# A 34,267-instruction, two-block transformer kernel: the first score products of four attentions placed between projections, and the last mixer's compressed scores computed with the keys stationary

## The reference, cut to what matters

```
# cross_attn, twice: 4 heads of 256
q = xn @ wq;  sc = q k^T * 256**-0.5;  p = softmax(sc);  o = p v;  h = h + o @ wo
# even_mixer_2: q, k (rotated), v for 8 causal heads, and 4 heads with two softmax maps each
qa, ka, va, qb, kb, vb = split(h @ w_in);  w = p[:, 0] - lam * p[:, 1]
# odd_mixer: 16 query heads, 4 key heads; three branches added under learned gates
s_c = q kc^T   # kc, vc: 15 compressed blocks, two small matrix products over 32 tokens each
p_c = softmax(mask(s_c));  o_c = p_c vc
o = g0 * o_c + g1 * o_selected + g2 * o_window
```

## Time and profile before

| | us |
|---|---|
| three runs | 2513.89, 2507.85, 2509.01 |
| median | 2509.01 |
| span of the profiled execution | 2503.7 |
| PE busy in it | 2362.8 |

### The profile page before, as it was taken

One profiled execution on the slowest core, in us unless ns is written; L12 is line 12 of the kernel. 1 busy time (PEld: TensorE's weight loads), 2 busy tenths in 40 slices (PEclk: granted clock), 3 DMA queues, 4 the chain that ended last, 5 costly groups with the idle time before them and its releaser, 6 DMA issues.

```text
span 2503.7 us, 34267 instructions
## 1 busy us (share of the span) xinstructions
PE 2362.8 (94%) x14928; PEld 1345.4 (54%) x14928; DVE 685.4 (27%) x1507; ACT 379.2 (15%) x812; POOL 1.2 (0%) x9
## 2 busy tenths in 40 slices
PE   7899999999999999989998999988979997989997
PEld 6767888877676333323333333335656334856433
DVE  2565122149555110101010101001142122263122
ACT  2002100010221111101110111101032111153212
POOL 0000000000000000000000000000000000000000
PEclk9899999999999999999998999998989998989999
DMA  9588154564374998999999999998402996542591
GB/s 314 185 299 313 68 215 155 194 220 140 108 262 178 351 382 330 390 370 393 394 393 393 394 394 359 387 370 328 146 34 72 324 339 168 146 135 73 194 346 50
DMA packets 328739, 645.07 MB, mean 258 GB/s; under 512 B 12907, under 2 KB 98177, under 8 KB 328577
## 3 DMA queue, kind: packets, MB, share of 16 engines
q1 hardware_dynamic: 325804, 637.63, 70.9%
q10 hardware_dynamic: 2773, 5.11, 0.6%
HBM read 641.66 MB, written 1.05 MB: 257 GB/s over the span
## 4 chain that ended last, share of the span: by engine, by line
PE 88%; DVE 7%; issue 3%; ACT 2%; ACTq 0%; DVEq 0%
PE bank L1579 22%; PE bank L1274 19%; PE bank L1644 11%; PE bank L1544 6%; PE bank L1498 6%; PE bank L1510 3%; PE bank L1571 3%; PE bank L1294 3%; DVE att L3276 2%; PE bank L1704 2%; PE bank L1663 1%; PE bank L1630 1%; PE bank L1790 1%; PE bank L1323 1%; PE bank L1724 1%
## 5 line engine op out<-in xcount | busy, mean ns | idle before, releaser
L1579 PE MATMUL bank<-ring,xn 128*32 128x512 f32 x3648 | 469.7, 595 | 0.0
L1274 PE MATMUL bank<-xn,ring 128*128 128x256 f32 x2048 | 451.8, 382 | 2.9 <-issue 1.0
L1274 PEld LDWEIGHTS bank<-xn,ring 128*128 128x128 f32 x2048 | 390.9, 192 | 60.7 <-issue 7.8
L1579 PEld LDWEIGHTS bank<-ring,xn 128*32 128x32 f32 x3648 | 128.6, 110 | 273.7 <-issue 270.0
L1644 PE MATMUL bank<-ring,att 128*32 128x512 f32 x2256 | 254.4, 593 | 1.3 <-ACT att L2326 1.3
L2883 DVE TENSOR_TENSOR sq<-att,bank 32x512 f32<-32x512 f32 x70 | 48.0, 686 | 501.2 <-ACT att L2337 351.9
L1544 PE MATMUL bank<-ring,xn 128*64 128x512 f32 x304 | 146.1, 627 | 28.2 <-issue 28.2
L1644 PEld LDWEIGHTS bank<-ring,att 128*32 128x32 f32 x2256 | 72.8, 110 | 162.5 <-issue 162.1
L1498 PE MATMUL bank<-xn,ring 128*128 128x256 f32 x704 | 152.8, 379 | 0.0
L1546 PE MATMUL bank<-ring,xn 128*64 128x512 f32 x304 | 147.3, 632 | 0.0
L1498 PEld LDWEIGHTS bank<-xn,ring 128*128 128x128 f32 x704 | 133.8, 190 | 18.3
(11 more groups left out here) (351 smaller groups left out, 2142.2 us busy)
## 6 DMA issues: line engine op xcount, KB each, us to landing
ring<-od_moe_gu SPq DMA_DIRECT2D x98, 2048.0 KB, 17.6
ring<-od_moe_down SPq DMA_DIRECT2D x49, 2048.0 KB, 15.6
ring<-ada_w SPq DMA_DIRECT2D x24, 2048.0 KB, 8.8
ring<-moe_w_gate SPq DMA_DIRECT2D x32, 1024.0 KB, 10.8
ring<-moe_w_up SPq DMA_DIRECT2D x32, 1024.0 KB, 10.5
ring<-moe_w_down SPq DMA_DIRECT2D x16, 2048.0 KB, 13.6
z<-od_moe_gu SPq DMA_DIRECT2D x14, 2048.0 KB, 18.7
ring<-ev_w_in SPq DMA_DIRECT2D x10, 2048.0 KB, 19.8
```

The source lines that it names most:

```text
L1274: mm = nc.tensor.matmul(ps[:, c * T:(c + 1) * T], kblk(b)[:, k, u * T + c * P:u * T + (c + 1) * P], x[:, k, :], start=k == 0, stop=k == KD ...
L1579: return nc.tensor.matmul(PSB[f.b][j * QP:(j + 1) * QP, :], src[:, k, at:at + QP], kblk(b)[:, k, :], start=k == 0, stop=k == KD - 1)
```

## The change

In both cross-attentions a score pass stands behind the next unit of the query projection, so that units and passes alternate on PE; ACT's copies and exponentials and DVE's `ada_step`s, reductions and normalisations alternate in the same way. In the even mixer the projections come in the order qa, ka, qb, kb, va, vb, the first unit's scores stand between the two halves of va and the second unit's ahead of vb; the wait for the last rotation is replaced by a wait of each unit for its own. The rotation's temporary moves from `sq` to `att`. In the last mixer the first unit's scores stand ahead of the `cmp_w2` products, the compressed scores are made as 8 products with the 32 key columns stationary and 256 query columns moving, in four column strips of a bank, ACT copies them, PE goes on with the second unit's scores, and four transposes bring the compressed scores into the layout of before. The score banks there become two fixed sets, (6, 7, 4) and (0, 1, 4), so that all units use bank 4 for the early tile. `turn_compressed` moves behind `turned(0)`.

```diff
-                j.s_fill, j.t_fill = fill((0, 1, 6)[i % 3]), fill(2 + i % 2, (probT_ready, count(probT_ready, 1) + 1))
+                j.s_fill, j.t_fill = fill((6, 7, 1)[i % 3]), fill(2 + i % 2, (probT_ready, count(probT_ready, 1) + 1))
...
+        SCORE_PAIRS = (6, 7, 4), (0, 1, 4)
...
+                freed = (score_ready, st.score + 3 * u.i + 3)
+                u.early_fill = fill(at[2], freed) if len(at) > 2 else fill_turn(freed)
+
+            def score_banks(u):
+                return pairs[u.i % 2] if pairs else [SCORE_BANKS[(3 * u.i + k) % 5] for k in range(3)]
...
         MW = MOBA_H * HD
-        ev2.ropes = [rope_linear(W2, 0, MW), rope_linear(W2, MW, MW)]
-        ev2.va = token_linear(W2, 2 * MW, MW, proj_ready)
-        ev2.ropes += [rope_linear(W2, 3 * MW, MW), rope_linear(W2, 4 * MW, MW)]
-        ev2.vb = token_linear(W2, 5 * MW, MW, proj_ready)
-        ev2.lam_fill = fill_turn()
...
-        ev2.att = maps(units, (att, kT.rearrange("p k t -> p (k t)")))
+        ev2.ropes = [rope_linear(W2, at * MW, MW) for at in (0, 1, 3)]
+        ev2.lam_fill = fill_turn()
+        ev2.ropes.append(rope_linear(W2, 4 * MW, MW))
+        ev2.att = maps(units, (att, kT.rearrange("p k t -> p (k t)")), begun=True)
+        ev2.va = token_linear(W2, 2 * MW, MW, proj_ready)
+        ev2.att.score_fills(units[0], (6, 7))
+        ev2.att.score_fills(units[1], (6, 7))
+        ev2.vb = token_linear(W2, 5 * MW, MW, proj_ready)
+        ev2.att.rest()
+        for i, u in enumerate(units):
+            u.rotated = (rope_ready, ev2.ropes[1 if i < 2 else 3].rope + i % 2 + 1)
+            u.projected = (proj_ready, (ev2.va if i < 2 else ev2.vb).end)
...
             u.evac = (slice(0, T), mixed[:, i, :])
+            u.rotated, u.projected = (rope_ready, od2.q.rope + i // 2 + 1), None
             units.append(u)
-        od2.cturn = fill(TURN_BANKS[1], (csoft_ready, od2.csoft + 4))
-        od2.att = maps(units, (att, z[:, 8:14, :].rearrange("p k t -> p (k t)")))
+        od2.att = maps(units, (att, z[:, 8:14, :].rearrange("p k t -> p (k t)")), begun=True, pairs=SCORE_PAIRS)
+        od2.att.score_fills(units[0], SCORE_PAIRS[0])
+        for i, st in enumerate(od2.cmp):
+            st.out = count(cmp_ready, 2)
+            st.ofill = fill_turn((cmp_ready, st.out + 2))
+        od2.csoft = count(csoft_ready, 4)
+        od2.by_block = fill(5, (blockwise_ready, 1))
+        od2.att.score_fills(units[1], SCORE_PAIRS[1])
+        od2.cscore = fill(5, (csoft_ready, od2.csoft + 1))
+        od2.att.rest(lambda: fill(TURN_BANKS[1], (csoft_ready, od2.csoft + 4)))
...
-            def pe_attention(st):
+            def pe_attention(st, q_unit):
+
                 def scores(j):
+                    pe.wait_ge(*j.projected)
...
                 js = st.jobs
-                for j in js[:3]:
-                    scores(j)
+                for i in range(len(js)):
+                    q_unit(i)
+                    if i:
+                        scores(js[i - 1])
+                scores(js[-1])
                 for i, j in enumerate(js):
-                    if i + 3 < len(js):
-                        scores(js[i + 3])
                     turned(j)
                     if i:
                         values(js[i - 1])
                 values(js[-1])
...
-                pe_linear(st.q, xn, normed(st.norm))
-                pe.wait_ge(proj_ready, st.q.end)
-                pe_attention(st.att)
+
+                def q_unit(i):
+                    b, u, f = st.q.units[i]
+                    if u == 0:
+                        landed(b)
+                    unit(b, u, f, xn, normed(st.norm) if i == 0 else None)
+                    sums_beside(st.q, i)
+
+                pe_attention(st.att, q_unit)
...
             rotate(r[0], 0)
-            pe_token_linear(ev2.va, xn)
+            pe_linear(r[2], xn, None)
             rotate(r[1], 4)
-            pe_linear(r[2], xn, None)
-            pe_linear(r[3], xn, None)
-            rotate(r[2], 8)
-            pe_token_linear(ev2.vb, xn)
-            rotate(r[3], 12)
             pe.wait_ge(lam_ready, 1)
             ps = open_bank(ev2.lam_fill)
             nc.tensor.matmul(ps[:, 0:2], ones[0:1, :], lam[0:1, 6:8], start=True, stop=True)\
                 .then_inc(bank_full[ev2.lam_fill.b], 1)
-            pe.wait_ge(rope_ready, r[3].rope + 2)
-            pe.wait_ge(proj_ready, ev2.vb.end)
-            pe_maps(ev2.att)
+            pe_linear(r[3], xn, None)
+            rotate(r[2], 8)
+            scores, rest = pe_maps(ev2.att)
+            for i, (b, c, f) in enumerate(ev2.va.units):
+                if i == 0:
+                    landed(b)
+                else:
+                    scores(ev2.att.units[0])
+                token_unit(b, c, f, xn)
+            rotate(r[3], 12)
+            scores(ev2.att.units[1])
+            pe_token_linear(ev2.vb, xn)
+            rest()
...
+            scores, rest = pe_maps(od2.att)
+            pe.wait_ge(dup_ready, od2.kv[1].dup + 2)
+            scores(od2.att.units[0])
...
+            ps = open_bank(od2.by_block)
+            for half in range(2):
+                for q in range(4):
+                    i = 4 * half + q
+                    g = i // 2
+                    mm = nc.tensor.matmul(ps[q * QP:(q + 1) * QP, half * T:(half + 1) * T],
+                                          kcmp[:, g // 2, g % 2].rearrange("p h n -> p (h n)"), z[:, i, :],
+                                          start=True, stop=True)
+            mm.then_inc(bank_full[od2.by_block.b], 1)
+            scores(od2.att.units[1])
+            pe.wait_ge(blockwise_ready, 1)
             ps = open_bank(od2.cscore)
             for c in range(TC):
-                for i in range(NSA_H // 2):
-                    g = i // 2
-                    at = c * T + i * 2 * NCMP_PAD
-                    mm = nc.tensor.matmul(ps[:, at:at + 2 * NCMP_PAD], z[:, i, c * P:(c + 1) * P],
-                                          kcmp[:, g // 2, g % 2].rearrange("p h n -> p (h n)"), start=True, stop=True)
+                for half in range(2):
+                    mm = nc.tensor.transpose(ps[:, c * T + half * P:c * T + (half + 1) * P],
+                                             raw_cmp[:, half, c * P:(c + 1) * P], ident)
             mm.then_inc(bank_full[od2.cscore.b], 1)
-            pe.wait_ge(dup_ready, od2.kv[1].dup + 2)
...
-            pe_maps(od2.att, turn_compressed)
+                mm.then_inc(bank_full[od2.att.second.b], 1)
+
+            rest(turn_compressed)
...
                 js = st.jobs
+                q_unit(0)
+                q_unit(1)
                 exps(js[0])
+                q_unit(2)
                 exps(js[1])
+                q_unit(3)
...
             copy_units(r[0], pairs(z), HD ** -0.5)
             copy_units(r[1], pairs(z, 4))
-            copy_units(ev2.va, tokens())
             copy_units(r[2], pairs(z, 8), HD ** -0.5)
             copy_units(r[3], pairs(z, 12))
+            exps, rest = act_maps(ev2.att)
+            copy_unit(ev2.va, tokens(), 0)
+            exps(ev2.att.units[0])
+            copy_unit(ev2.va, tokens(), 1)
+            exps(ev2.att.units[1])
             copy_units(ev2.vb, tokens(MW))
-            act_maps(ev2.att)
+            rest()
...
+            nc.scalar.copy(flat_cmp, full(od2.by_block)).then_inc(blockwise_ready, 1)
+            exps, rest = act_maps(od2.att)
+            exps(od2.att.units[0])
             act.wait_ge(csoft_ready, od2.csoft + 1)
             nc.scalar.activation(flat_cmp, flat_cmp, ACT.Exp).then_inc(csoft_ready, 1)
+            exps(od2.att.units[1])
 
             def turned_compressed():
-                nc.scalar.copy(pT_cmp.rearrange("p h t -> p (h t)"), full(od2.cturn)).then_inc(csoft_ready, 1)
-
-            act_maps(od2.att, turned_compressed)
+                nc.scalar.copy(pT_cmp.rearrange("p h t -> p (h t)"), full(od2.att.second)).then_inc(csoft_ready, 1)
+
+            rest(turned_compressed)
...
                 js = st.jobs
+                beside(0)
+                beside(1)
                 scores(js[0])
+                beside(2)
                 scores(js[1])
-                for i, j in enumerate(js):
-                    if i + 2 < len(js):
-                        scores(js[i + 2])
-                    probs(j)
-
-            def dve_maps(st, second=None):
+                probs(js[0])
+                beside(3)
+                scores(js[2])
+                probs(js[1])
+                scores(js[3])
+                probs(js[2])
+                probs(js[3])
...
+            ev2_tmp = att[:, 8 * T:10 * T].rearrange("p (c t) -> p c t", c=2)
+            rotary(ev2.ropes[0], 0, ev2_tmp)
+            rotary(ev2.ropes[1], 4, ev2_tmp)
             f = ev2.lam_fill
             nc.vector.tensor_copy(lam[:, 0:2], full(f)[:, 0:2]).then_inc(bank_free[f.b], 1)
             freed(f)
-            dve_maps(ev2.att)
+            rotary(ev2.ropes[2], 8, ev2_tmp)
```

(14 more changed lines are left out.)

151 lines of the change are left out of this document (79 added, 72 removed).

## The result

The changed kernel takes 2495.94 us (median of 4 runs, 2492.41 to 2497.54); before, beside it, 2511.45 (2507.85 to 2518.54). The ratio is 0.9932, with a 95% interval of 0.9912 to 0.9953: faster by 0.7%. The difference of the medians is 15.5 us; 15.7 were forecast, but two of the terms were off by some 2 to 4 us each, in opposite directions.

A forecast was written before the change was run, and what follows sets the result against it. PE, busy in 94% of the span, was taken as the bound, leaving its idle time and low-clock stretches to win. Gains of 2.4 + 0.8 + 10.0 + 2.5 = 15.7 us made 2509.0 into 2493.3 us, range 2486 to 2501.

The forecast's parts named there:

- First cross-attention: Score passes between query units hide PE's waits; of 2.96 us idle 0.6 is left, gain 2.4 us.
- Second cross-attention: Three waits become one of 4.6 us, followed by 6.2 us at 1.2 GHz; gain 0.8 us.
- I count all: Experts behind the second cross-attention: the cross-attentions' gains are taken to reach the end of the program in full.
- The rival: The experts, with DMA saturated, swallow both cross-attentions' gains: gain 12.5 us, time 2496.5; chance 0.08.
- Even mixer: Score passes among projections at full clock, last rotation hidden, waits of 1.6 and 1.3 us left; gain 10.0 us.
- a case that the prediction had priced at up to 2.5: Even mixer: the clock falls all the same after the two waits left, and 2.5 us go.
- these waits are shorter than those after which the clock fell: Even mixer: the waits left, 1.6 and 1.3 us, were held too short to follow earlier falls of the clock.
- Last mixer: Strips take 1.3 us, a new wait of 8.1 us for bank 4 precedes scores(2), then lower clock; gain 2.5 us.
- the lower clock for 6.2 to 9.0 us: Last mixer, after the new wait: PE at 1.2 GHz this long, with scores(2) taking 4.9 us.
- the rivals on the clock: After the new waits the lower clock lasts longer (2500.2 us, chance 0.14) or the clock does not fall (2486.9, 0.10).
- The slower case: Last mixer: after 8.1 us idle, short products never bring the full clock back; 2544 us, chance 0.03.

The follow-up runs named there:

- e2: The kernel before with only the even mixer's part of the change; ratio 0.9974 to before.
- e7: The changed kernel with the sum of the second cross-attention's fourth modulation block moved behind the last probabilities; 2484.59 us, ratio 0.9894 to before.
- e3: The kernel before with only the last mixer's part of the change; ratio 0.9982 to before.
- e8: The changed kernel with 7 products of zeros in PE's routing wait ahead of the first experts; 2483.57 us, ratio 0.9887 to before.
- e12: The changed kernel with the edits of e6, e7 and e8 together; 2474.82 us, ratio 0.9843 to before.
- e5: The changed kernel with DVE's scores(1) moved ahead of probs(0) in the last mixer; ratio 0.9914 to before.
- e6: The changed kernel with 33 products of zeros in PE's wait ahead of scores(2) in the last mixer; ratio 0.9916 to before.
- e4: The changed kernel with the compressed scores in the old form, 32 products moving 32 columns each, without ACT's copy and the four transposes; ratio 0.9926 to before.
- e10: The changed kernel with the edits of e5, e7 and e8, and 20 products of zeros in the wait e5 leaves; 2471.09 us, ratio 0.9836 to before.
- e11: The changed kernel itself, run and profiled again with nothing altered; 2492.37 us, ratio 0.9927 to before.
- e9: The changed kernel with 7 more products of zeros in PE's idle time at the very start of the program; 2484.18 us.

## Why the prediction was right, point by point

**First cross-attention: right.** 2.4 forecast, 33.94 - 31.31 = 2.63 measured. All profiles with the change have 31.31 or 31.32; of the three without it two have 33.9, and e2 has 35.50, with the clock at 0.50 behind the old form's wait of 1.58 us. 0.48 us of waiting is left, 0.6 was forecast: 0.22 in the place that was named, behind ACT's copy, and 0.26 ahead of the second job's transposes, which wait for DVE and for which the sum had nothing.

**Second cross-attention: right in its place.** One wait of 4.41 us (4.6 forecast), and a gain of 40.82 - 39.93 = 0.89 (0.8), with the clock at 0.50 behind it; in half of the profiles the low clock was shorter and the gain 2.3. e7 shows both causes as put: with DVE's step moved the wait and the low clock are gone.

**"I count all": this step failed.** From the sums in the second attention to the even mixer's first rotation it is 1055.1 us (mean of before, e2 and e3) and, with the change, 1056.3 (mean of seven): 0.8 was counted as won and 1.2 are lost. The rival named this place, but with the wrong mechanism: DMA. If late loads had taken the gain, they would have taken e7's as well, and e8's 2. What is shown is a routing wait of 1.94 us that was there before too. Behind it the clock stayed at full in the three profiles of the old attentions and fell in all that have the changed ones with their wait of 4.4 us (e8, where it is filled, apart), at a cost of 0.35 to 2.0 us; in e7, without the long wait, it did not fall. The rest lies late in the experts: from the end of the last long wait ahead of an expert's weights to the first product of the next stage it is 23.8 us in the three profiles with the old attentions and 25.1 to 26.2 in the seven with the changed ones, with the clock at 0.50 behind that wait in the seven alone. The wait in the attention is not needed for that: e12, which has neither that wait nor the one for the routing, took 26.7. Why it falls there in one execution and not in another stays open.

**Even mixer: right.** 10.0 forecast; 110.22 - 100.03 = 10.19 in seven of the eleven profiles, 8.6 in four. There the pass behind the wait of 1.69 us ran at the lower clock, a case that the prediction had priced at up to 2.5. The waits were 1.69 and 1.24 us (1.6 and 1.3), and the last value pass ended 24.5 us after vb (25). But the forecast was wrong that these waits are shorter than those after which the clock fell. The trace of before has one as short, ahead of scores(3) of the last mixer, with a granted clock of 0.50 over 2225.5 to 2228.5:

```profile
2225.45 0.58 PE L1403 MATMUL bank<-zeros 128*128 128x512 bf16 x1 [1.69 <-ACT sq L2270]
```

**Last mixer: mechanism right, one term mis-sized.** The strips took 1.07 us (1.3), the wait 7.87 (8.1), DVE ended it, for bank 4 (e5), and the clock fell because PE was idle (e6). But I took "the lower clock for 6.2 to 9.0 us" from two stretches in which the clock had fallen at most 0.5 us before the wait ended. Here it fell at about 2203.9, 6.2 us ahead of scores(2), so most of the 10.2 us at 0.50 passed while PE stood, and 4.1 were left (3.2 to 4.2 in the six profiles with this wait). scores(2) took 4.4 us (4.9), all that follows ran at full clock, and scores(4) came 5.2 us earlier instead of 2.5. Against the mean of the old stage (75.23, 77.30, 76.45) the gain is 6.4. In those three the clock fell 0.6 to 2.3 us ahead of the old form's short products and stood at 0.50 for 10 to 17 us; that these products hold it low is likely by e4, but not shown for those three.

So the sum of the means is 2.6 - 1.2 + 9.4 + 6.4 = 17.2; the ratio makes 17.1 of 2511.45 us (11.8 to 22.1), the medians 15.5. The last mixer gave 2 to 4 us more than forecast, and the stretch behind the second attention took 2 back: that the total came out close is luck, as these cancel.

Of the rivals on the clock neither came true: it fell at both long waits, and stayed low behind them for as long as in the earlier trace rows in half of the profiles of the second attention and for a shorter time otherwise. The slower case, a clock that does not come back, was not seen.

## What to carry to other kernels

Price a moved step by the wait that it makes for the engine behind it, then look at what that engine still owes ahead of what frees the bank: here one DVE step in another order was worth 2 us in one place (e5) and 5.1 to 6.6 in the other (e7), where the change itself had won 0.9 to 2.3. Products of zeros in a wait that can't be removed kept the clock in e6 and e8, and cost nothing while they were shorter than the wait; but two remedies for one wait need not add (e10). A gain of 1 to 3 us is read from its own stretch in several profiles, not from the time of the whole program.

## What the runs showed of the hardware that was not expected

- The length of a wait does not set how long the clock stays at 0.50 behind it: 4.1 us behind 7.87, 6.2 or 3.2 behind the same 4.41 (changed, e11), 6.7 (the forecast read 6.2) behind 2.68 and 9.7 behind 3.06 (before). Part of the reason is that in the wait of 7.87 us the clock had fallen 6.2 us before work came back. The Trainium skill, "TensorE: Matmul & The Clock Gate", section "What's actually happening", says that the number of products at the lower clock at the start of a kernel changes from run to run. e11 agrees, in the middle of a kernel: 3.75 and 3.08 us for the same 8 records.
- The clock fell to 0.50 under products that move 32 columns each, with PE busy all the time (e4, 2195 to 2199), while 16 records of 256 columns for the same scores kept it at 1.00.
- Seven products more, in either of two places ahead, removed a break of 5 to 8 us on PE that no engine and no transfer ended (e8, e9), and with it 7 to 9 us of the time. That PE waits there for its own program to be loaded is only argued from this; what is shown is that the break keeps its place in the program.
